# Half of the branch gates computed in the merge instead of within attention, in a one-core transformer kernel

## The reference

```python
# first block, in short
h = rms_norm(x, norm_mix_w) * (1 + scale1) + shift1        # scale, shift: c_act @ ada_w + ada_b
aq, ak, av, hq, hz_f, hz_b, hi, hgate, gate_logits = split(h @ w_in)
o_att = attention(rope(rms_norm(aq)), rope(rms_norm(ak)), av)     # 8 heads, 2 key heads
o_hg  = rms_norm(gated_scan_forward + gated_scan_backward) * silu(hgate)   # 4 heads
ya, yh = o_att @ w_branch_att, o_hg @ w_branch_hg
g = sigmoid(gate_logits)                                   # 2 branches x 1024, from 2048 columns of w_in
merged = g[0] * ya + g[1] * yh
x = x + gate1 * (merged @ w_out)
h = rms_norm(x, norm_ffn_w) * (1 + scale2) + shift2
x = x + gate2 * expert_choice_ffn(h)                       # 16 experts, 64 tokens each, 24 MB of weights each
```

## Time and profile before

| | us |
|---|---|
| median of 3 runs | 2258.07 |
| lowest and highest of them | 2257.34, 2259.25 |
| the profiled execution, its own time | 2251.97 |
| span from its first to its last instruction | 2250.2 |
| mean granted clock of TensorE in it | 0.966 of full |

### The profile page before, as it was taken

One profiled execution on the slowest core, in us unless ns is written; L12 is line 12 of the kernel. 1 busy time (PEld: TensorE's weight loads), 2 busy tenths in 40 slices (PEclk: granted clock), 3 DMA queues, 4 the chain that ended last, 5 costly groups with the idle time before them and its releaser, 6 DMA issues.

```text
span 2250.2 us, 19571 instructions
## 1 busy us (share of the span) xinstructions
PE 2005.9 (89%) x8422; PEld 1117.0 (50%) x8422; DVE 606.8 (27%) x868; ACT 412.6 (18%) x621; POOL 32.7 (1%) x42
## 2 busy tenths in 40 slices
PE   3986999999987998889998889888889998999996
PEld 2543465534663433434343334333334477888785
DVE  4152336532022111010101011111128613222233
ACT  2123545510020100000000000000020213222222
POOL 0000000000000000000000000000030000000000
PEclk9998999999898999999999999999999999999998
DMA  8210023344424999999999999999952122233210
GB/s 333 75 38 19 1 75 114 130 150 149 187 96 182 416 416 417 417 416 416 416 415 416 416 416 416 415 416 416 417 187 75 38 75 94 94 95 104 83 38 38
DMA packets 143787, 513.37 MB, mean 228 GB/s; under 512 B 7891, under 2 KB 70355, under 8 KB 107731
## 3 DMA queue, kind: packets, MB, share of 16 engines
q1 hardware_dynamic: 141632, 503.35, 57.3%
q10 hardware_dynamic: 2070, 8.78, 1.0%
HBM read 510.00 MB, written 2.10 MB: 228 GB/s over the span
## 4 chain that ended last, share of the span: by engine, by line
PE 71%; DMA 18%; DVE 5%; ACT 4%; issue 1%; SPq 0%; POOL 0%; ACTq 0%; DVEq 0%; POOLq 0%
PE ps L416 15%; DMA work<-in_w_exp_up 13%; PE ps L924 11%; PE ps L888 7%; PE ps L421 6%; PE ps L1067 5%; DMA ring<-in_w_exp_up 4%; PE ps L1026 4%; PE ps L1028 4%; PE ps L1027 4%; PE ps L846 3%; PE ps L626 3%; PE ps L571 1%; DMA ring<-in_ada_w 1%; PE ps L869 1%
## 5 line engine op out<-in xcount | busy, mean ns | idle before, releaser
L888 PE MATMUL ps<-work 128*64 128x512 f32 x1256 | 351.6, 595 | 40.3 <-DMA work<-in_w_exp_up 40.3
L416 PE MATMUL ps<-work,ring 128*128 128x512 f32 x784 | 344.6, 598 | 0.8 <-DVE work L1597 0.8
L888 PE MATMUL ps<-ring,work 128*64 128x512 f32 x792 | 242.6, 595 | 23.7 <-DMA ring<-in_w_exp_up 23.7
L416 PEld LDWEIGHTS ps<-work,ring 128*128 128x128 f32 x784 | 149.0, 192 | 187.9 <-issue 186.3
L888 PEld LDWEIGHTS ps<-work 128*64 128x64 f32 x1256 | 116.0, 137 | 230.3 <-issue 154.0
L1767 DVE TENSOR_TENSOR work<-work,ps 64x512 f32<-64x512 f32 x64 | 42.0, 691 | 503.7 <-ACT work L1329 503.1
L1329 ACT ACTIVATE work<-ps 64x512 f32<-64x512 f32 x64 | 32.6, 585 | 758.3 <-PE ps L888 758.3
L888 PEld LDWEIGHTS ps<-ring,work 128*64 128x64 f32 x792 | 80.5, 137 | 128.1 <-issue 82.3
L421 PE MATMUL ps<-ring,work 128*128 128x256 f32 x640 | 141.3, 383 | 2.5 <-DVE work L1664 1.7
L924 PE MATMUL ps<-work 128*64 128x512 f32 x600 | 140.0, 618 | 3.7 <-issue 3.1
L1026 PE MATMUL ps<-xh,wh 128*128 128x512 f32 x352 | 138.0, 392 | 1.0 <-issue 1.0
(11 more groups left out here) (236 smaller groups left out, 1878.5 us busy)
## 6 DMA issues: line engine op xcount, KB each, us to landing
work<-in_w_exp_gate SPq DMA_DIRECT2D x80, 1024.0 KB, 23.2
work<-in_w_exp_up SPq DMA_DIRECT2D x77, 1024.0 KB, 23.2
work<-in_w_exp_down SPq DMA_DIRECT2D x75, 1024.0 KB, 20.8
ring<-in_w_exp_down SPq DMA_DIRECT2D x53, 1024.0 KB, 21.2
ring<-in_w_exp_up SPq DMA_DIRECT2D x51, 1024.0 KB, 22.4
ring<-in_w_exp_gate SPq DMA_DIRECT2D x48, 1024.0 KB, 22.6
ring<-in_w_in SPq DMA_DIRECT2D x27, 1024.0 KB, 5.6
ring<-in_ada_w SPq DMA_DIRECT2D x24, 1024.0 KB, 6.0
```

The costliest lines, as they stand in the source:

```text
L416: i = e.matmul(bank(bk), piece(key)[:, off + k, 128 * j:128 * j + 128], rhs(k), start=(k == 0), stop=(k == nk - 1))
L888: i = e.matmul(PS[64 * gu:64 * gu + 64, fb, :], at(XET + 128 * k + 64 * z, 64), flat(key)[:, 512 * fb:512 * fb + 512], start=(k == 0), sto ...
```

## The change

Gates for the columns `h` = 1 are no longer computed in the attention stretch but in the merge, in the way in which those of `h` = 2 and 3 are. The pieces `("bg", 1, 0)` and `("bg", 1, 1)` become `("c0", 1)` and `("c1", 1)`. `branch_gates` has four gates instead of eight, all four with rooms in `TMP`, and the weave names `fill` twice instead of four times. Slot 3 is a weight slot again: the dense weights cycle over slots 0 to 3, the modulation weights over 4 and 5. Behind that the experts' cycle of slots is the former one with each ring slot's number raised by one. The late gates of the merge begin at `d` = 2. The instructions themselves are the same in number, apart from ScalarE's table loads.

```diff
@@ ring_plan
-    bg = [("bg", h, br) for h in range(2) for br in range(2)]
-    ada = lambda i: [(("ada", 8 + 2 * i), 4), (("ada", 9 + 2 * i), 5)]
-    more = [(bg[0], 0)] + ada(0) + [(bg[1], 1), (bg[2], 2)] + ada(1) + [(bg[3], 0)] + ada(2)
-    rest = [("cb", 0), ("cb", 1), ("c0", 2), ("c1", 2), ("cb", 2), ("c0", 3), ("c1", 3), ("cb", 3)]
-    for i, key in enumerate(rest):
-        more += [(key, (1, 2, 0)[i % 3])] + (ada(3 + i) if i < 5 else [])
-    more += [(("wo", n), (3, 4, 5, 0)[n]) for n in range(4)]
...
+    ada = lambda i: [("ada", 8 + 2 * i), ("ada", 9 + 2 * i)]
+    more = [("bg", 0, 0)] + ada(0) + [("bg", 0, 1)] + ada(1) + ada(2) + [("cb", 0)] + ada(3)
+    for half in (1, 2, 3):
+        more += [("c0", half), ("c1", half)] + (ada(2 + 2 * half) if half < 3 else []) + [("cb", half)] + (ada(3 + 2 * half) if half < 3 else [])
...
+    slots += [4, 5, 0, 1]
...
-    cycle = (8, 11, 12, 13, 14, 10, 9, 1, 2, 7, 3, 4, 5, 0, 6)
+    cycle = (8, 11, 12, 13, 14, 10, 9, 2, 3, 7, 4, 5, 0, 1, 6)
@@ build
-        def rooms(x, kept=SLOT[3]):
-            return kept + 512 * x if x < 4 else TMP + 512 * (x - 4)
+        def rooms(x):
+            return TMP + 512 * x
@@ sync
-                if key == ("wo", 0):
-                    e.wait_ge(s["mg_m"], 4)
@@ tensor (scalar and vector alike)
             def branch_gates():
-                for x in range(8):
-                    key = ("bg", x // 4, x // 2 % 2)
+                for x in range(4):
+                    key = ("bg", 0, x // 2)
...
-            weave(fill, lv, fill, att, fill, att, fill)
+            weave(fill, lv, att, fill, att)
...
             for d in range(8):
...
-                if d >= 4:
+                if d >= 2:
                     k0, k1 = ("c0", half), ("c1", half)
...
-                    e.wait_ge(s["bg_a"], 8)
+                    e.wait_ge(s["bg_a"], 4)
@@ scalar, merge
-            for d in range(4, 8):
-                i = d - 4
+            for d in range(2, 8):
+                i = d - 2
```

More of the change, by code:

```diff
@@ L109, in ring_plan @@
     slots = [i % 6 for i in range(len(keys))]
-    bg = [("bg", h, br) for h in range(2) for br in range(2)]
-    ada = lambda i: [(("ada", 8 + 2 * i), 4), (("ada", 9 + 2 * i), 5)]
-    more = [(bg[0], 0)] + ada(0) + [(bg[1], 1), (bg[2], 2)] + ada(1) + [(bg[3], 0)] + ada(2)
-    rest = [("cb", 0), ("cb", 1), ("c0", 2), ("c1", 2), ("cb", 2), ("c0", 3), ("c1", 3), ("cb", 3)]
-    for i, key in enumerate(rest):
-        more += [(key, (1, 2, 0)[i % 3])] + (ada(3 + i) if i < 5 else [])
-    more += [(("wo", n), (3, 4, 5, 0)[n]) for n in range(4)]
-    keys += [key for key, _ in more]
-    slots += [slot for _, slot in more]
+    ada = lambda i: [("ada", 8 + 2 * i), ("ada", 9 + 2 * i)]
+    more = [("bg", 0, 0)] + ada(0) + [("bg", 0, 1)] + ada(1) + ada(2) + [("cb", 0)] + ada(3)
+    for half in (1, 2, 3):
+        more += [("c0", half), ("c1", half)] + (ada(2 + 2 * half) if half < 3 else []) + [("cb", half)] + (ada(3 + 2 * half) if half < 3 else [])
+    n = m = 0
+    for key in more:
+        if key[0] == "ada":
+            slots.append(4 + m % 2)
+            m += 1
+        else:
+            slots.append(n % 4)
+            n += 1
+    keys += more + [("wo", n) for n in range(4)]
+    slots += [4, 5, 0, 1]
     ex = []
@@ L344, in last_reader @@
             if kind == "c0":
-                return s["mg_ga"], 2 * key[1] - 2
+                return s["mg_ga"], 2 * key[1]
             if kind == "c1":
-                return s["mg_gb"], 2 * key[1] - 2
+                return s["mg_gb"], 2 * key[1]
             if kind == "cb":
```

41 lines of the change are left out of this document (18 added, 23 removed).

## The result

The changed kernel takes **2268.88 us** (median of four runs, 2267.13 to 2269.7) beside 2257.7 for the kernel before (four runs of the same session, 2254.12 to 2259.25). The ratio is 1.0056, with a 95% interval from 1.0041 to 1.0072: slower by 11.2 us at the medians, 0.5%. The prediction was 2267.4 us.

A forecast was written before the change was run, and what follows sets the result against it. TensorE was taken to bound attention and merge, transfers the experts. The 27.5 us moved cancels; 9.3 us of new attention waits added to the median 2258.07 gave 2267.4 us, range 2260 to 2275.

The forecast's parts named there:

- Work moved at equal price: 32 gate matmuls leave full attention for the full merge: 27.5 us off one, 27.5 us onto the other.
- The round: Late attention: a round of 11.96 us falls to some 9.5, being 8.52 of TensorE work plus a 1.05 us wait.
- the head gate: First attention round: sigmoid, product and table loads stand between the second head gate and what follows, 0.4 us of wait.
- The wait for the diagonal copies: First attention round: ScalarE does two diagonal copies ahead of the transposes' copy, so TensorE waits 0.4 us.
- The ring and its last link: Attention rounds: scores, maximum, exponential, key copy, level; TensorE waits 1.05 us for ScalarE's key copy, VectorE needs 9.1 us.
- Work passed on one for one: Experts' stage is bound by transfers and keeps its length; attention's and merge's joint gain or loss reaches the end unchanged.
- What was costed at nothing: Weight slots, rooms, late gates at `d` = 2 and 3, dropped `("wo", 0)` wait, renamed experts' slots: 0 us.
- the clock falls: Rival, attention rounds: waits drop TensorE's clock to 1.2 GHz, 1.9 us per fall, three falls, +15 us in total; chance 0.17.
- sum of 9.3 us: New TensorE waits in attention: first round 1.8, second level 2.0, third 1.3, four more at 1.05 making 4.2.
- The load's draining of 1.38 us: Skill page's extra cost behind each ScalarE table load; would delay four rounds' exponentials 1.4 us, making the waits 15 us.

The follow-up runs named there:

- e2_copyfirst: Changed kernel with ScalarE's key copies of six levels placed ahead of the newest exponential instead of behind it; 2264.94 us, ratio 1.003.
- e3_fillahead: Changed kernel with both fill steps of a late attention round ahead of the level on all three engines; 2278.13 us, ratio 1.0106.
- e5_short_ada: Changed kernel with early key copies and VectorE's modulation products cut to 128 of 2048 columns in seven of eight steps; 2259.77 us, ratio 1.001.
- s1_pad: Kernel before with one gate product of the merge made four times, 20.6 us more TensorE work; 2279.5 us, ratio 1.0096.
- s2_pad: Kernel before with one gate product of the merge made twice, 6.9 us more TensorE work; 2265.29 us, ratio 1.0041.
- e1_tail: Changed kernel with the tail's slots handed on one place, so one early second-block weight piece follows the last down pieces, not two; 2268.61 us, ratio 1.0063.
- e6_hold: Kernel before with the second-block weight piece behind the last down piece held back on SyncE until that piece is used up; 2252.91 us, ratio 0.9995.
- k1_warm: Changed kernel with three useless TensorE matmuls added around the last expert's waits ahead of its down products; 2266.92 us, ratio 1.0045.
- a0_after: The changed kernel run again without edits, on another chip; 2267.12 us, ratio 1.0061 against the kernel before.
- e7_hole: Kernel before with TensorE's waits between attention and merge filled by a value product and one merge gate product moved there; 2254.33 us, ratio 0.9982.
- b1_holewarm: Kernel before with the waits ahead of the merge filled by moved products, plus three useless matmuls in the last expert; 2249.95 us, ratio 0.9987.

## Why the prediction was right, point by point

**Work moved at equal price: right.** 27.5 predicted for the merge, 27.47 measured.

**The round: right in kind and nearly in size.** 9.5 us predicted, 9.66 to 9.79 measured. The waits ahead of the four late levels are 0.90 to 1.03 (1.05 predicted), ahead of the second 1.50 (2.0), ahead of the third 1.03 (1.3), ahead of the first 0.69 (1.0), for the head gate 0.44 (0.4). The wait for the diagonal copies (0.4) did not occur. In sum **7.5 in place of 9.3**: the terms that were mis-sized are those of the first three rounds, which I had counted hand-over by hand-over on VectorE and ScalarE. But a wait costs more than itself. Without waits a round takes 8.52 us (e2_copyfirst), and with 0.97 us of wait it takes 9.73, some 0.25 more than the two together. The four records of the gate ahead of the level give way to it after 1.82 us where no wait stands between (372.32 to 374.14 in e2_copyfirst), and run out in 1.98 where one does; the level is 0.07 longer. Seven times 0.25 are 1.7 us, an estimate from the late rounds, so waits and hand-overs make 9.2. The hand-overs are a term that the prediction did not have. Attention and merge together gave +8.1, since one value product met a shorter slow stretch (5.3 against 6.1 us); the other 0.3 us I can't place. ScalarE lost six table loads in the stretch (16 left of 22), where the prediction counted eight; nothing hung on it.

**The ring and its last link: right, shown.** e2_copyfirst takes the waits away by moving the copy, e3_fillahead makes them longer by putting a load and a sigmoid ahead of it, and e2_copyfirst shows VectorE as the next bound, at rounds of 9.0 us, which the prediction had counted as 9.1; with less work on VectorE (e5_short_ada) they take 8.53.

**Work passed on one for one: right.** The experts' stage kept its length, and s1_pad and s2_pad pass on 20.6 and 6.9 us as 21.5 and 7.3.

**What was costed at nothing.** Slots, rooms, `("wo", 0)`'s wait and the late gates cost nothing, as said: one wait in the merge, none for a transfer. I came to doubt the renamed experts' slots when the last down products were 2.2 us longer. e1_tail, e6_hold and k1_warm clear them: the products are long with two pieces, one or none beside them, and take 10.52 us with two when part of the waits is filled.

**The step that the runs correct: the clock.** The rival *the clock falls* was placed in attention's rounds, and there it did not come true: the rounds ran at the full clock with a wait of 1 us in each. It came true where the prediction did not look, in stages that the change does not touch: in the last down products, in `w_out_2`'s and near the end, 5.4 us together. By its times and mean clocks the kernel before has these falls in 42 of 74 executions. Another 2.2 us come between the modulation rows and the experts (2.2 in a0_after too). In the first profile more of modulation's narrow products run slow there, and the 48 behind them take 23.48 us in place of 22.56. The rival's price of 1.9 us for a fall is a little high besides: it set a second level of 2.61 us beside a late one of 1.95, and a second level takes 2.09 at the full clock.

**Where it was luck.** The forecast met the time because it added the 9.3 us to the median of the runs and not to the profiled execution; 2261.3, the sum on the profiled execution, would have been 6 to 8 us low, since that execution was of the kernel's lower group and the changed kernel had none there in nine. The three runs behind that median were all of the upper group; on two of the four chips the median of before was 2252.1 and 2253.7. And errors in the sum of 9.3 us cancel: it has 1.8 us of waits too much, and lacks 1.7 of hand-overs and 2.2 of slower products ahead of the experts. The stretch that was changed gave 8.1, not 9.3.

**The Trainium skill's two places.** The load's draining of 1.38 us (the Trainium skill, page "ScalarE: Activation LUTs", section "What ACT_TABLE_LOAD costs") did not show: a round with a sigmoid and its two loads lasts 9.79 us, one without them 9.66. The clock that falls and rises with short idle times (the Trainium skill, page "TensorE: Matmul & The Clock Gate", section "A second HAM failure mode: psum-queue depth-cycling") did not show for the seven waits of 0.7 to 1.5 us in attention, and did show behind the last expert's waits of 0.82 and 0.98 us, where filling part of them kept the clock at 1.00.

## What to carry to other kernels

Independent work that fills the busiest engine's time within a ring of dependent steps is free to move only as long as enough stays to cover the ring. Here half of it was taken out, and a round is now as long as the ring, 9.7 us for 8.5 of work, while the work that left is paid in full where it goes. Look for waits that are already there, as the 5.9 us between attention and merge, and move work into these. And before a difference of a few microseconds behind the changed place is put down to the change, compare the same place in two executions of one program: here the clock alone makes 5 us.

## What the runs showed of the hardware

- TensorE's same instructions, alike within 0.1 us up to 1629 us, ran on at a granted clock of 1.00 in one execution (before) and 0.55 in the other (e6_hold, which differs in one wait of SyncE). The times of 74 executions of one kernel fall into two groups, with mean clocks of 0.965 to 0.968 and 0.960 to 0.964. Small waits open the way to a fall, and do not decide it.
- Three useless matmuls of 2.15 us in all, two of them in waits of 0.82 and 0.52 us, kept the clock up, though a wait of 0.97 us between them remained, and made 48 products 10.52 us long in place of 12.65, a net gain of 1.9 us at that place.
- 1 MB transfers beside the last down pieces made no difference to the matmuls: at the low clock 12.7, 12.8 and 12.6 us with two, one and none (a0_after, e1_tail, e6_hold), at the full one 10.52 with one and with two (before, k1_warm).
- What filling a gap wins can be lost to the clock further on, in one execution and not in the next: 6.9 us won by e7_hole at 539 us were some 4 at 582, and 7.5 at 578 in b1_holewarm, with the same instructions up to there.
